# Scan copies, block carry, conv weight tables, state bounce and residual loads rearranged in a hybrid conv/S5 encoder block

## What is computed

```python
z = rms_norm(h);  p = z @ w_in            # [conv value | conv gate | S5 input]
u = v * sigmoid(gate)                     # conv group, 512 channels
y = depthwise_conv(u, width 31) + b
conv_out = silu(layer_norm(y))
# S5: 32 groups x 16 channels, 64 complex states each, both directions
bu = einsum('gph,blgh->blgp', b_bar, x)
s  = associative_scan(a_r * a_l, a_r * b_l + b_r)
y  = gelu(sum of both directions of Re(C s) + D * x)
ssm_out = y * sigmoid(y @ glu_w + glu_b)
h = h + concat(conv_out, ssm_out) @ w_out
h = h + relu(rms_norm(h) @ w_ff1)^2 @ w_ff2
out = rms_norm(h)
```

## Time and profile before

| what | value |
|---|---|
| device time, 3 runs | 920.38 us median (920.36 to 921.90) |
| the profiled execution's own time | 922.01 us |
| its span, slowest core (core 1) | 921.0 us; the cores take 914.0 to 921.0 us |
| PE busy | 784.7 us (85% of the span) |
| DVE, ACT, POOL busy | 500.5, 363.2, 400.2 us |
| chain that ended last, by engine | PE 68%, waits for issue 8%, DVE 7%, ACT 7%, DMA 5%, POOL 3%, SP's queue 2% |
| granted TensorE clock, core 1 | 0.942 of 2.4 GHz |
| DMA | 87.27 MB, mean 95 GB/s |

### The profile page before, as it was taken

The page is one execution under the profiler, slowest core; times in us unless marked ns, Lnnn a source line. Parts: engine busy times, 40 slices in busy tenths (PEclk is TensorE's granted clock), DMA queues, the critical chain, the costliest instruction groups (busy, mean ns, idle before and its releaser), DMA issues.

```text
span 921.0 us, 15729 instructions; the slowest of 8 cores (914.0 to 921.0 us)
## 1 busy us (share of the span) xinstructions
PE 784.7 (85%) x4584; PEld 390.0 (42%) x4584; DVE 500.5 (54%) x963; ACT 363.2 (39%) x588; POOL 400.2 (43%) x454
## 2 busy tenths in 40 slices
PE   1457577689966996789999999999999999999992
PEld 0233244345434565235544444444444444444440
DVE  5747975837778845436643343343343343343487
ACT  5878876433124455736631111111111111111453
POOL 3877994846789616000043324324323323323220
PEclk9978979799987898779999999999999999999997
DMA  8478875353459575699051410605024050410134
GB/s 231 149 200 240 181 171 135 59 92 45 61 86 105 52 138 143 181 251 249 2 73 21 61 31 1 93 1 92 1 20 74 1 92 0 61 32 1 47 138 183
DMA packets 71955, 87.27 MB, mean 95 GB/s; under 512 B 7584, under 2 KB 55840, under 8 KB 71872
## 3 DMA queue, kind: packets, MB, share of 16 engines
q1 hardware_dynamic: 56752, 66.18, 30.5%
q0 software_dynamic: 14400, 19.76, 13.9%
q10 hardware_dynamic: 720, 0.33, 0.1%
HBM read 86.56 MB, written 19.45 MB: 115 GB/s over the span
## 4 chain that ended last, share of the span: by engine, by line
PE 68%; issue 8%; DVE 7%; ACT 7%; DMA 5%; POOL 3%; SPq 2%; DVEq 0%; ACTq 0%; POOLq 0%
PE p_pb L1143 24%; PE p_pb L1163 23%; PE p_pb L1089 6%; PE p_pb L1012 3%; PE p_pb L448 3%; DVE p_pb L477 2%; SPq L162 2%; DMA scr_uc<-s_usc 2%; ACT s_zt L349 2%; PE p_pb L843 1%; PE p_pb L931 1%; ACT s_wb L640 1%; PE p_pb L942 1%; PE p_pb L944 1%; DMA s_braw<-bmat 1%
## 5 line engine op out<-in xcount | busy, mean ns | idle before, releaser
L477 DVE TENSOR_TENSOR s_h<-s_h,p_pb 128x512 f32<-128x512 f32 x288 | 197.5, 687 | 260.7 <-PE p_pb L1163 246.2
L477 POOL TENSOR_TENSOR s_hid<-s_rl 128x512 bf16<-128x512 f32 x128 | 133.7, 1048 | 322.4 <-ACT s_rl L1151 318.0
L1163 PE MATMUL p_pb<-s_w2c,s_hid 128*128 128x512 bf16 x1024 | 226.8, 379 | 4.1 <-DVE s_h L477 4.1
L1143 PE MATMUL p_pb<-s_zf,s_w1c 128*128 128x512 bf16 x1024 | 226.4, 379 | 0.0
L1151 ACT ACTIVATE s_rl<-p_pb 128x512 f32<-128x512 f32 x128 | 76.0, 596 | 327.8 <-PE p_pb L1143 315.4
L1163 PEld LDWEIGHTS p_pb<-s_w2c,s_hid 128*128 128x128 bf16 x1024 | 99.4, 98 | 126.5 <-issue 7.9
L1143 PEld LDWEIGHTS p_pb<-s_zf,s_w1c 128*128 128x128 bf16 x1024 | 100.2, 98 | 120.0
L448 PE MATMUL p_pb<-s_zsl,s_winu 128*128 128x512 bf16 x256 | 73.0, 439 | 9.2 <-ACT s_ust L462 8.6
L372 PE MATMUL p_pb<-s_ident,s_zt 128*128 128x128 bf16 (+1 forms) x264 | 26.7, 261 | 46.1 <-ACT s_zt L358 33.1
L843 PE MATMUL p_pb<-s_zsl,s_winv 128*128 128x512 bf16 x256 | 57.9, 387 | 2.8 <-DVE s_usc L859 1.6
L448 PEld LDWEIGHTS p_pb<-s_zsl,s_winu 128*128 128x128 bf16 x256 | 27.0, 111 | 43.2 <-issue 26.0
(11 more groups left out here) (168 smaller groups left out, 938.6 us busy)
## 6 DMA issues: line engine op xcount, KB each, us to landing
s_xt<-xl SPq DMA_DIRECT2D x32, 512.0 KB, 6.3
s_h<-xl SPq DMA_DIRECT2D x16, 512.0 KB, 17.0
s_w1c<-w_ff POOLq DMA_DIRECT2D x8, 1024.0 KB, 11.9
s_w2c<-w_ff POOLq DMA_DIRECT2D x8, 1024.0 KB, 11.6
out<-s_h SPq DMA_DIRECT2D x15, 512.0 KB, 2.7
s_wstv<-w_in SPq DMA_DIRECT2D x4, 1024.0 KB, 9.0
s_kf<-scr_rs SPq DMA_DIRECT2D x8, 384.0 KB, 18.2
s_wstu<-w_in SPq DMA_DIRECT2D x4, 512.0 KB, 11.2
```

The lines of the kernel that those rows point to most:

```text
L477: op(eng, lambda e: e.tensor_tensor(o, a, b_, op=o_), r=r, w=w)
L1143: op("pe", lambda e, k=k, f=f: e.matmul(pb[pi_][:, :], w1c[fc % 2][:, k, f * 128:(f + 1) * 128], zf[:, k, b * 512:(b + 1) * 512], start=(k ...
L1163: op("pe", lambda e, f=f, half=half: e.matmul(pb[pi_][:, :], hid[hb][:, f, ti * 128:(ti + 1) * 128], w2c[fc % 2][:, f, half * 512:(half + ...
```

## The change

Five edits, in the order in which they run.

- **Copies.** ACT takes both halves of the pairs 10 to 15, DVE the second halves of the pairs 0 to 9. That is 22 copies on ACT and 10 on DVE, in place of 20 and 12.
- **Carry.** The 15 borders are taken as four runs of four: one copy, two steps for all four runs at once, one for three, then three single steps from run to run with the power for four borders (index 8 of the table), and three steps for all runs. On each engine that is 38 operations in place of 61, some of them on four times (or three times) the elements.
- **Conv weight tables.** All 38 carry operations of DVE are mixed with the tables 0, 1 and 2; the conv loop makes none before pair 0. `bbf`, which the strips read, is moved from under table 2's buffer, and `sgt1` and two `ysq` buffers move too.
- **State bounce.** After each call of `ssm_out` four groups (256 KB) are written, and the four groups of the call before are read back in four DMAs of 64 KB.
- **Residual rows.** `resid_load` issues on POOL's queue, the first one when the last read of `mixc`'s chunk 1 is in.

```diff
+    bbf = sm("bbf", [128, NU * 32 + 16], BF16)
     BBO = smp[0]
     bbar = sm("bbar", [128, NU, 2, 16], F32)
-    bbf = sm("bbf", [128, NU * 32 + 16], BF16)
...
-            if x == 0 or i % 4 == 3:
+            if x == 0 or i >= 10:
...
-            x1, x2 = [t[:, 0:nu * 2].rearrange("p (u r) -> p u r", u=nu) for t in (self.x1, self.x2)]
...
-            for b in range(15):
...
-                tt(eng, x1, src, pr.unsqueeze(2).to_broadcast([128, nu, 2]), ALU.mult, [ck, "cx", kr], [self.k1])
-                tt(eng, x2, src[:, :, ::-1], pi, ALU.mult, [ck, "cx", ki], [self.k2])
-                tt(eng, dst, xb, x1, ALU.add, self.vk + [self.k1], [ck])
-                tt(eng, dst, dst, x2, ALU.add, [ck, self.k2], [ck])
+            X7 = self.X[:, :, :, 7, :]
+            def run(src, dst, xb, n, pr, pi, kr, ki):
+                y1, y2 = [t[:, 0:nu * 2 * n].rearrange("p (u r s) -> p u r s", u=nu, r=2) for t in (self.x1, self.x2)]
+                tt(eng, y1, src, pr.unsqueeze(2).unsqueeze(3).to_broadcast([128, nu, 2, n]), ALU.mult, [ck, "cx", kr], [self.k1])
+                tt(eng, y2, src[:, :, ::-1, :], pi.unsqueeze(3).to_broadcast([128, nu, 2, n]), ALU.mult, [ck, "cx", ki], [self.k2])
+                tt(eng, dst, xb, y1, ALU.add, self.vk + [ck, self.k1], [ck])
+                tt(eng, dst, dst, y2, ALU.add, [ck, self.k2], [ck])
...
+            op(eng, lambda e: e.tensor_copy(C[:, :, :, 1::4], X7[:, :, :, 0::4]), r=tt_keys, w=[ck])
+            for i in (1, 2):
+                run(C[:, :, :, i::4], C[:, :, :, i + 1::4], X7[:, :, :, i::4], 4, pr, pi, kr, ki)
+            run(C[:, :, :, 3:12:4], C[:, :, :, 4:13:4], X7[:, :, :, 3:12:4], 3, pr, pi, kr, ki)
+            p4r, p4i = pxre[:, 8, self.u0:self.u1], pximx[:, 8, self.u0:self.u1]
+            for s in range(3):
+                run(C[:, :, :, 4 * s:4 * s + 1], C[:, :, :, 4 * s + 4:4 * s + 5], C[:, :, :, 4 * s + 4:4 * s + 5], 1, p4r, p4i, "pxre", "pximx")
+            for i in range(3):
+                run(C[:, :, :, i::4], C[:, :, :, i + 1::4], X7[:, :, :, i::4], 4, pr, pi, kr, ki)
...
-    sgts = [sb("sgt%d" % i, [128, 512], F32, (SG, CMO)[i]) for i in range(2)]
+    sgts = [sb("sgt%d" % i, [128, 512], F32, (SG, CMO + 1024)[i]) for i in range(2)]
...
-    ysq = [sb("ysq%d" % i, [128, 2, 256], F32, (SG, CMO)[i // 2] + 2048 * (i % 2)) for i in range(4)]
+    ysq = [sb("ysq%d" % i, [128, 2, 256], F32, (SG, PWO)[i // 2] + 2048 * (i % 2)) for i in range(4)]
...
+    def ys_write(i):
+        P.dma("sp", bass.AP(scr["ys"], 4 * i * 128 * 256, [[256, 128], [128 * 256, 4], [1, 256]]), gs[:, 4 * i:4 * i + 4, :],
+              r=["gs%d" % i], w=["scr_ys%d" % i])
+    def ys_read(i):
+        c = i // 2
+        for gl in range(4 * (i % 2), 4 * (i % 2) + 4):
+            P.dma("sp", mixs[16 * gl:16 * gl + 16, c, :].rearrange("p (t k) -> p t k", t=8),
+                  bass.AP(scr["ys"], (8 * c + gl) * 128 * 256, [[256, 16], [16 * 256, 8], [1, 256]]),
+                  r=["scr_ys%d" % i], w=["mixs%d_%d" % (c, gl)])
...
-    for c in range(4):
-        P.place("gs%d" % c, "gs", VV1 + 4096 * c, 4096)
+    for i in range(8):
+        P.place("gs%d" % i, "gs", VV1 + 2048 * i, 2048)
...
-               r=[pbk[bi]], w=["gs%d" % (pp0 // 4)])
+               r=[pbk[bi]], w=["gs%d" % (pp0 // 2)])
...
-        P.dma("sp", h[:, t, :], _rows(xl, 2 + 128 * (t % 2), t // 2), w=["h%d" % t])
+        P.dma("pool", h[:, t, :], _rows(xl, 2 + 128 * (t % 2), t // 2), r=["mixc1_7"] if t == 0 else [], w=["h%d" % t])
...
-    dq = zipped([dq[:24], ops_of(lambda: [cd_gen(0), cd_gen(1)])]) + dq[24:]
+    dq = zipped([dq, ops_of(lambda: [cd_gen(0), cd_gen(1), cd_gen(2)])])
...
-        if i % 2 == 0 and i // 2 + 2 < 8:
+        if i % 2 == 0 and i >= 2 and i // 2 + 2 < 8:
...
-        if i % 2 == 1:
-            c = i // 2
-            back_write("ys", gs, "gs%d" % c, c)
-            if c > 0:
-                back_read("ys", c - 1, mixs, "mixs%d" % (c - 1))
+        ys_write(i)
+        if i > 0:
+            ys_read(i - 1)
...
-    back_read("ys", 3, mixs, "mixs3")
+    ys_read(7)
```

More of the change, by code:

```diff
@@ L798, in carry @@
             pr, pi, kr, ki = self.tab(7)
-            x1, x2 = [t[:, 0:nu * 2].rearrange("p (u r) -> p u r", u=nu) for t in (self.x1, self.x2)]
             op(eng, lambda e: e.memset(C[:, 0::2, :, 0:1], 0.0), r=["cx"], w=[ck])
-            for b in range(15):
-                src, dst, xb = C[:, :, :, b], C[:, :, :, b + 1], self.X[:, :, :, 7, b]
-                tt(eng, x1, src, pr.unsqueeze(2).to_broadcast([128, nu, 2]), ALU.mult, [ck, "cx", kr], [self.k1])
-                tt(eng, x2, src[:, :, ::-1], pi, ALU.mult, [ck, "cx", ki], [self.k2])
-                tt(eng, dst, xb, x1, ALU.add, self.vk + [self.k1], [ck])
-                tt(eng, dst, dst, x2, ALU.add, [ck, self.k2], [ck])
+            X7 = self.X[:, :, :, 7, :]
[5 more added lines that the diff above has]
+                tt(eng, dst, dst, y2, ALU.add, [ck, self.k2], [ck])
+            tt_keys = self.vk + ["cx"]
+            op(eng, lambda e: e.tensor_copy(C[:, :, :, 1::4], X7[:, :, :, 0::4]), r=tt_keys, w=[ck])
[7 more added lines that the diff above has]
+                run(C[:, :, :, i::4], C[:, :, :, i + 1::4], X7[:, :, :, i::4], 4, pr, pi, kr, ki)
         def corr(self, sk, u0, u1):
```

## The result

| what | before | after |
|---|---|---|
| device time | 921.14 us median (4 runs) | 937.27 and 939.77 us |
| ratio | | 1.019, 95% interval 1.0165 to 1.0216 |
| profiled execution | 922.01 us | 937.27 us |
| span, slowest core (core 1 in both) | 921.0 us | 936.2 us |
| DVE, ACT, POOL busy | 500.5, 363.2, 400.2 us | 504.5, 364.5, 406.9 us |

All ratios compare undisturbed runs only; two further runs of the changed kernel were disturbed and are left out. The kernel became 17.5 us slower (1.9% of 921.1), where 4.6 us were forecast.

A forecast was written before the change was run, and what follows sets the result against it. The bound was the chain to the output projection: conv waiting for table 3, SP's queue, the last `mixc` landing. -8.1 - 3.9 + 16.6 = +4.6 us on 922.0, carried to a 925.0 us median; range 907 to 929.

The forecast's parts named there:

- contention: Before the output projection: residual rows on GpSimd's queue hold up the later `mixc` reads, +16.6 us.
- 1408 packets, 22.7 us at 62 per us: Time for the 11 `mixc` reads caught by the residual rows, 128 packets each; last one through at 399.3.
- The rule of one for one: Two queues sharing the DMA engines are served packet for packet, whatever their size, 55 of each per us.
- (a): Rival at the `mixc` reads: small reads slip in between residual packets, full 12.0 us gained, 908.4 us; chance 0.20.
- (b): Rival: residual loads start late, first packet 4.7 us after issue, six reads caught, -3.0, 917.4 us; chance 0.16.
- State bounce: On SP's queue behind the S5 output: eight `mixs` reads are left instead of 16, 3.9 us gained.
- SP has until the last call to catch up, so I count nothing: First state writes meet the tail of the `w_out` load; cost counted as nothing, 0 to 1.5 us.
- Conv: Table 3 comes earlier, the wait before pair 6 shrinks from 6.47 to some 0.5 us; 8.1 gained, 2.7 from the clock.
- Carry on GpSimd: GpSimd's carry takes 15.7 us instead of 20.5; by itself the edit costs and gives nothing.
- Rival (c): 96-element GpSimd operations take 0.6 us, table 4 is late for pair 8, conv gain 5.6, 927.5 us; chance 0.12.
- the cover of the other: Without GpSimd's new carry, table 4 would come at 301.0 and PE would wait 1.5 us before pair 8.
- Copies: ACT's two more copies delay the start of the scan and conv input by 0.5 us (0 to +1.0).

The follow-up runs named there:

- e1: The changed kernel with the residual rows put back on SP's queue behind the `mixc` reads; ratio 0.9962 to the kernel before, 919.5 us.
- e13: The changed kernel with only the first four residual tiles issued after `mixc`'s chunk 1, the others after the last `mixc` read; ratio 1.0044, 926.5 us.
- e7: e1 with DVE's corrections swapped, units 16 to 19 before units 0 to 15; ratio 0.9880 to the kernel before, 912.4 us.
- e6: e1 with the fourth-power tables of the single carry steps copied to PSUM for DVE; ratio 0.9914 to the kernel before.
- e12: e7 with the old carry (15 borders in turn, 61 operations on either engine); ratio 0.9936 to the kernel before.
- e2: The kernel before with one edit alone, the residual rows issued on GpSimd's queue after `mixc`'s chunk 1; ratio 1.0254.

## Why the prediction was wrong

- **The direction and the main mechanism, contention, were right, the size was not**: +17.5 us instead of +4.6, outside the range. Of the 12.9 us by which core 1's stages miss the sum, 7.8 are the contention, 2.5 the state bounce, and 2.6 the stretch up to the S5 output.
- **Contention, predicted 16.6, measured 24.4** (20.8 in the median core). Each term but one held nearly. The first residual packet came 2.2 us after the issue on core 1 (2.0 taken; 1.3 to 2.2 over the cores). 1457 packets were caught (1408 predicted). Nine tenths of them went at 62 per us (62 predicted; median of the cores 66). The step that failed is "1408 packets, 22.7 us at 62 per us": it divides a total by a mean rate. The last tenth took another 8.0 us, where the rate gives 2.3: that is 5.7 of the 7.8 us. The 49 packets more are 0.8, and the rest is that the first residual packet came earlier, seen from where the last read would have landed. The final norm's `gfin` load stands behind the `mixc` reads in SP's queue; its first packet runs at 400.3 us, while the last `mixc` packet is at 410.3, so some of the 16 DMA engines were through 10 us before the slowest. The trace shows it directly: every DMA leaves sixteen completion signals. Those of the last `mixc` read come from 400.70 to 410.87, the last two 3 us behind the others, and PE goes on at 411.00; in e1 they come from 384.57 to 385.07. Over the cores they are 3.7 to 12.1 us apart in the changed kernel, and 1.9 to 5.0 in e13, so this tail goes with the mixture. Why the engines differ is open.
- **The rule of one for one held**, and rivals (a) and (b) fell: the queues moved 1500 and 1480 packets. The Trainium skill, DMA: Bandwidth & Descriptors, Queues, rings and completion order, says that each DMA engine goes round its queues packet by packet, on rings of its own. The trace agrees in both: equal counts, and signals that come 10 us apart. The page's packet is a group of descriptors, and here the trace can't tell a turn of one record from a turn of a group, since a `mixc` read and a residual tile have 128 data records each.
- **State bounce, predicted -3.9, measured -1.4** (in the seven profiles with this code also -1.4 in the median of all cores, 7.6 for 9.0). The step "SP has until the last call to catch up, so I count nothing" failed. The loads of `w_out` and `glu_w` ran until about 340 us. The first write was issued at 332.66, but its first packet moved only at 336.56; for 3.9 us the loads alone had the DMA engines, and this was no sharing one for one. It was 3.0 to 4.3 us on the seven cores where `w_out` still had packets to move, and 0.9 on core 5, where it had none; the kernel before, where `w_out` was through or within 0.5 us of it, has 0.9 to 1.2. Then the write shared with the load of `glu_w`, and SP waited for its landing until 341.37. Why a queue gets no turn at first is open. From there SP needs 2.5 us for a call and PE and ACT 3.27, so that it makes up 0.8 us in each; the last write was still 3.0 us behind the last GELU. e7 confirms it: with `w_out` through or nearly so (first packet after 0.9 to 1.6 us) all 3.9 us are gained. The prediction had seen the collision and bounded it at 1.5 us.
- **Conv, predicted -8.1, measured -5.5 on core 1 from the same starting event** (from the block states to the S5 output, 129.4 to 123.9), and -2.9 in the median core (126.8 to 123.9). The clock's part (2.7) was right; the earlier trace rows and the fence above show it. Two steps failed. A carry operation on 160 elements takes 0.44 us, not 0.32. And the single steps read their power table in SBUF, which I had counted at 0.28 like the others. DVE by form, 255.6 to 282.8 us, core 1 of after (compare):

```profile
L477 DVE TENSOR_TENSOR p_pb<-s_cx,p_pb 128x160 f32<-128x160 f32 x8 | 3.3, 441 | 0.2
L477 DVE TENSOR_TENSOR p_pb<-s_cx,s_pximx 128x40 f32<-128x40 f32 x3 | 2.9, 961 | 0.0
...
L477 DVE TENSOR_TENSOR p_pb<-s_cx,s_pxre 128x40 f32<-128x40 f32 x3 | 1.9, 627 | 0.2
```

  Both make DVE late between the strips (PE waits 2.92 and 2.18 us for `s_rs`), a place that the prediction didn't name: six list operations follow each strip set, and the conv waits for the last strip. The conv started 1.7 us later, against +0.65 forecast; e6, without the slow multiplications, has 1.1 of it back (74.5 to 73.4).
- **Carry on GpSimd** took 16.7 us (241.12 to 257.82), 15.7 predicted and 20.5 before. Rival (c) fell, and the claim that this edit is the cover of the other was right: e12 removes it and waits 3.5 us.
- **Copies**: +0.5 predicted, +0.5 in the median (12.35 against 11.8 us from the block states to the first full product of the conv input).
- **Behind the output projection** nothing moved, as said: 15.3 us at its start and 15.2 in the span.
- The comparison of absolute times within one profile was a fault of method that also spoiled my first expectation (e1). Part of what looked like a match with the forecast (S5 output near 325.6, seen at 326.1) was the earlier start of that execution.

## What to carry to other kernels

A second queue is no free lane: if a chain of small transfers sets the end, bulk loads with large packets must be issued when the last small one has been issued or has landed, since both queues got equal numbers of packets here and the slowest DMA engine decides. Price such a mixture by the packets of the competitor and add about a quarter for the slowest engine (27.5 us here, where 1472 packets at 66 per us are 22.3; 28.7 in e2, where 1468 at 63 are 23.3; both with the same loads). Before moving a load or a write earlier, look at what else is on the DMA engines then; here the order of two lists on DVE freed the memory for a weights' load 7 us sooner and gave 7.6 us by the times and 3.4 by the stages, about as much again as the four other edits together (3.5 and 3.9). Measure stages from event to event on all cores, not from the start of the span on one.

## What the runs showed of the hardware that was not expected

- DVE's multiplication of 128 x 40 with both operands in SBUF took 0.63 and 0.96 us in the mean beside GpSimd's work, up to 1.03, against 0.22 with one operand in PSUM; with the tables in PSUM (e6) all took 0.22. The Trainium skill, SBUF — State Buffer, Who interferes with whom, says that a DVE instruction with two SBUF inputs contends with a GpSimd instruction that reads SBUF; the trace agrees: GpSimd's operations of that time are 0.83 to 1.03 us long, and a DVE multiplication that starts at 263.56 beside one (263.43 to 264.46) ends at 264.53, just behind it.
- The sixteen completion signals of one 64 KB read came 10.2 us apart in a mixture of 29 us (core 1; 12.1 on core 6), and 0.5 without the mixture (e1).
- A write issued on SP's queue while GpSimd's queue was moving a weights' load had its first packet 3.0 to 4.3 us after its issue (seven cores), against 0.9 to 1.2 where that load was about through.
- A load of 128 rows of 2 KB shows 64 packet records of 4 KB.
